# Key compression of a three-layer kernel with its blocks stationary in 64x32 tiles, and 1 MB of late weights loaded earlier

## What is computed

```python
def compress(kv, w1, w2, pe):                    # CMP_BLOCK 32, CMP_STRIDE 16, Dh 64, G 2
    B, T, G, Dh = kv.shape
    nc = (T - CMP_BLOCK) // CMP_STRIDE + 1       # 15 blocks
    idx = jnp.arange(nc)[:, None] * CMP_STRIDE + jnp.arange(CMP_BLOCK)[None, :]
    blocks = kv[:, idx] + pe[None, None, :, None, :]
    blocks = jnp.swapaxes(blocks, 2, 3).reshape(B, nc, G, CMP_BLOCK * Dh)
    return jax.nn.gelu(blocks @ w1) @ w2         # w1 is 2048 x 128, once for keys, once for values

def second_block(...):
    ...
    kc = compress(k_c...); vc = compress(v_c...)
    h = h + mix @ w_out[i]
    h = h + moe(rmsnorm(h, ln2[i]), w_router[i], ...)                               # 32 experts, top 4
    h = h + (p[i] @ w_ple[i]) * jax.nn.sigmoid(rmsnorm(h, ln_ple[i]) @ w_ple_gate[i])   # the last embedding
    return rmsnorm(h, ln_f)
```

## Time and profile before

| | |
|---|---|
| median of 3 runs | 1890.81 us (1889.72 to 1892.59) |
| profiled execution, own time | 1888.31 us |
| its span in the profile | 1886.4 us |
| TensorE busy with matmuls | 1733.7 us (92%) |
| VectorE / ScalarE busy | 744.8 us (39%) / 460.9 us (24%) |
| bytes moved | 549.43 MB, 291 GB/s over the span |
| granted TensorE clock, mean | 0.962 of full |

### The profile page before, as it was taken

The page is one execution under the profiler, slowest core; times in us unless marked ns, Lnnn a source line. Parts: engine busy times, 40 slices in busy tenths (PEclk is TensorE's granted clock), DMA queues, the critical chain, the costliest instruction groups (busy, mean ns, idle before and its releaser), DMA issues.

```text
span 1886.4 us, 23728 instructions
## 1 busy us (share of the span) xinstructions
PE 1733.7 (92%) x9692; PEld 1095.8 (58%) x9692; DVE 744.8 (39%) x1138; ACT 460.9 (24%) x725; POOL 13.1 (1%) x19
## 2 busy tenths in 40 slices
PE   8999999899999999999999889888898888977986
PEld 5799899797489989876544234333343333423332
DVE  3655567864365552153322222222222222213236
ACT  1544446522144441144222001000010100101003
POOL 0000000100000000000000000000000000000000
PEclk9999999999999999899899999999998999989998
DMA  9544443301354462213899999999999999999993
GB/s 395 211 196 196 192 154 135 134 1 77 146 234 179 178 232 113 80 45 132 331 428 427 428 428 428 428 428 425 429 428 429 428 427 428 428 427 428 427 428 160
DMA packets 41960, 549.43 MB, mean 291 GB/s; under 512 B 4824, under 2 KB 4984, under 8 KB 8728
## 3 DMA queue, kind: packets, MB, share of 16 engines
q1 hardware_dynamic: 39720, 540.45, 68.7%
q0 software_dynamic: 1872, 6.82, 1.0%
q10 hardware_dynamic: 288, 1.05, 0.1%
HBM read 545.12 MB, written 3.18 MB: 291 GB/s over the span
## 4 chain that ended last, share of the span: by engine, by line
PE 76%; DMA 17%; DVE 3%; ACT 2%; issue 1%; SPq 0%; DVEq 0%; ACTq 0%
DMA ring<-experts_dram 17%; PE ps L536 6%; PE ps L2186 6%; PE ps L2209 5%; PE ps L2231 5%; PE ps L2270 4%; PE ps L649 3%; PE ps L651 3%; PE ps L650 3%; PE ps L725 3%; PE ps L724 3%; PE ps L723 3%; PE ps L1241 3%; PE ps L2243 3%; PE ps L1456 2%; PE ps L2323 2%
## 5 line engine op out<-in xcount | busy, mean ns | idle before, releaser
L778 DVE TENSOR_TENSOR ring_split<-ring,ring_split 128x1024 fp32r<-128x1024 f32 x156 | 187.1, 1222 | 126.5 <-ACT ring_split L830 126.5
L2209 PE MATMUL ps<-ring,arena 128*32 128x512 f32 x1152 | 160.6, 709 | 81.6 <-DMA ring<-experts_dram 81.6
L2703 DVE TENSOR_SCALAR arena<-ps 128x512 f32<-128x512 f32 (+1 forms) x38 | 21.5, 566 | 495.1 <-PE ps L2209 201.4
L830 ACT CAST ring_split<-ring 128x1024 fp32r<-128x1024 f32 x156 | 160.6, 1047 | 165.0 <-PE ps L725 93.0
L2231 PE MATMUL ps<-ring,arena 128*128 128x512 f32 x384 | 168.6, 597 | 0.0
L3009 ACT ACTIVATE arena<-arena 128x512 f32<-128x512 f32 (+1 forms) x38 | 20.2, 530 | 574.6 <-DVE arena L2703 574.6
L2209 PEld LDWEIGHTS ps<-ring,arena 128*32 128x32 f32 x1152 | 42.0, 127 | 188.7 <-issue 182.5
L723 PE MATMUL ps<-arena_split,ring_split 128*128 128x256 f32 x512 | 145.3, 284 | 0.0
L725 PE MATMUL ps<-arena_split,ring_split 128*128 128x256 f32 x512 | 144.8, 283 | 0.0
L724 PE MATMUL ps<-arena_split,ring_split 128*128 128x256 f32 x512 | 144.4, 282 | 0.0
L2231 PEld LDWEIGHTS ps<-ring,arena 128*128 128x128 f32 x384 | 73.5, 192 | 88.8 <-issue 87.2
(11 more groups left out here) (435 smaller groups left out, 2501.3 us busy)
## 6 DMA issues: line engine op xcount, KB each, us to landing
ring<-experts_dram SPq DMA_DIRECT2D x192, 2048.0 KB, 20.0
ring<-weights_dram SPq DMA_DIRECT2D x55, 2048.0 KB, 11.4
row_buf<-rows_dram POOLq DMA_DIRECT2D x13, 512.0 KB, 9.0
ring<-heads_dram SPq DMA_DIRECT2D x4, 1024.0 KB, 4.8
ring<-weights_dram SPq DMA_DIRECT2D x3, 1024.0 KB, 11.5
tab<-tables_dram SPq DMA_DIRECT2D x1, 2160.5 KB, 31.4
tab<-weights_dram SPq DMA_DIRECT2D x1, 1536.0 KB, 25.7
gate_mid<-weights_dram SPq DMA_DIRECT2D x1, 1536.0 KB, 28.0
```

What stands on the lines that cost most here:

```text
L778: V.tensor_tensor(low, raw, high, ALU.subtract).then_inc(sem("part_low"), 1)
L830: A.copy(split_buffer(MLP_SPLIT_SLOT, buffer)[0], raw).then_inc(sem("part_high"), 1)
L2209: ins = T.matmul(view(bank(0)[TINY * q:TINY * q + TINY], (2, 256)), xs_of(4 * c + d, j)[:, 0:TINY], w[q // 2][:, d, :, 256 * (q % 2):256 * ...
```

## The change

Two edits. **First**, the operands of the compression's first product change places. The 32 columns of `cmp_in` of one position (30 blocks and 2 columns set to zero) are stationary, and the 128 columns of weights move. Keys and values use different row halves, and four successive positions use four different column groups of 32, so eight tiles of 64x32 take turns. Position `i` adds into partitions `32 * (i % 4)` onwards, so that four partial sums of 32x128 stand below one another. VectorE copies them out of PSUM (`cmp_part`), and a new `pe_compress_sum`, placed behind the first of the four outputs of the fox keys, adds the four and turns the result in one product for keys and one for values, with the table `own_expert` (1 where the partition modulo 32 is the column) moving. The gelu reads that result. **Second**, the load of the last embedding's weights stands ahead of the wait for `router_ids`, with a wait of its own for `router_psum`.

```diff
-        cmp_in = scratch(5696, 32, 30)
+        cmp_in = scratch(5696, 32, 32)
...
+        cmp_part = view(m_small[:, 0:256], (2, P))
...
             for r in range(4):
+                if r == 1:
+                    pe_compress_sum(pe)
                 m = turned(ps[:, 0, r * SEQ:(r + 1) * SEQ], w, 512, lambda a: a[:, r * P:(r + 1) * P])
...
-                    m = V.tensor_tensor(cmp_in[:, 16 * q:16 * q + 16, 15 * g:15 * g + 15], tokens_,
-                                        spread(pe_cols[:, 16 * q:16 * q + 16], 15), ALU.add)
-            m.then_inc(flag_up("cmp_in"), 1)
+                    V.tensor_tensor(cmp_in[:, 16 * q:16 * q + 16, 15 * g:15 * g + 15], tokens_,
+                                    spread(pe_cols[:, 16 * q:16 * q + 16], 15), ALU.add)
+            V.memset(cmp_in[:, :, 30:32], 0.0).then_inc(flag_up("cmp_in"), 1)
...
             V.tensor_copy(cumT, ps[0:8, 1, 512:768]).then_inc(sem("fox_cum"), 1)
+            v.wait_ge(*flag("cmp_part_psum"))
+            V.tensor_copy(cmp_part, view(ps[:, 3, :], (2, 512))[:, :, 0:P]).then_inc(flag_up("cmp_part"), 1)
...
             for i in range(32):
+                at = 32 * (i % 4)
                 for kv in range(2):
                     rows_ = slice(64 * kv, 64 * kv + 64)
-                    m = T.matmul(ps[:, 3, 512 * kv:512 * kv + 30], w[rows_, i * P:(i + 1) * P], cmp_in[rows_, i, :],
-                                 start=(i == 0), stop=(i == 31))
+                    m = T.matmul(ps[at:at + 32, 3, 512 * kv:512 * kv + P], cmp_in[rows_, i, :], w[rows_, i * P:(i + 1) * P],
+                                 start=i < 4, stop=i >= 28, skip_group_check=True)
+            m.then_inc(flag_up("cmp_part_psum"), 1)
+
+        def pe_compress_sum(pe):
+
+            pe.wait_ge(*flag("cmp_part"))
+            for kv in range(2):
+                m = T.matmul(ps[:, 3, 512 * kv + P:512 * kv + P + 32], cmp_part[:, kv, :], table("own_expert"), start=True, stop=True)
             m.then_inc(flag_up("cmp_hid_psum"), 1)
...
-                A.activation(hid[:, kv, :, 0:15], view(ps[:, 3, 512 * kv:512 * kv + 30], (2, 15)), ACT.Gelu_apprx_tanh)\
+                A.activation(hid[:, kv, :, 0:15], view(ps[:, 3, 512 * kv + P:512 * kv + P + 30], (2, 15)), ACT.Gelu_apprx_tanh)\
                  .then_inc(sem("cmp_hid"), 1)
...
                     sp.dma_start(parts[TILES + t], pre_low[t].bitcast(F32)).then_inc(sem("parts_kept"), 16)
+                sp.wait_ge(*flag("router_psum"))
+                sp.dma_start(w_ple2, weights[places["unit"]["ple2"], :, 0:2048]).then_inc(sem("ple2_loaded"), 16)
             sp.wait_ge(*flag("router_ids"))
             e = expert_at(TINY_1)
             for r, chunk in enumerate((A, B, A + 1, B + 1)):
                 load(CHUNKS + r, CHUNKS + r, e, chunk)
-            if n == 0:
-                sp.dma_start(w_ple2, weights[places["unit"]["ple2"], :, 0:2048]).then_inc(sem("ple2_loaded"), 16)
```

More of the change, by code:

```diff
@@ L46 @@
         "gdn_o1_psum", "att_kv_psum", "att_nat_psum", "att_qf_psum", "fox_cum_psum",
-        "cmp_hid_psum", "fox_rows1_psum", "cmp_kv_psum", "fox_rows0_psum", "cmp_score_psum", "cmp_pT_psum", "cmp_o_psum", "router_psum",
+        "cmp_part_psum", "cmp_hid_psum", "fox_rows1_psum", "cmp_kv_psum", "fox_rows0_psum", "cmp_score_psum", "cmp_pT_psum", "cmp_o_psum", "router_psum",
         "router_rank_psum", "router_wT_psum", "router_ids_psum", "router_sorted_psum",
@@ L52 @@
         "gdn_wT", "cmp_clear", "att_kv", "att_nat", "cmp_in", "fox_f", "fox_lf",
-        "cmp_hv4", "att_kf", "cmp_kcc", "cmp_vblk", "fox_bias", "cmp_diff", "cmp_prob", "cmp_pT", "cmp_o",
+        "cmp_part", "cmp_hv4", "att_kf", "cmp_kcc", "cmp_vblk", "fox_bias", "cmp_diff", "cmp_prob", "cmp_pT", "cmp_o",
         "router_top", "router_chosen", "router_rank", "router_weight", "router_perm", "router_wT", "router_ids",
```

## The result

The change takes 1881.07 us (median of 5 runs, 1878.98 to 1881.23), the kernel before 1890.60 beside it (5 runs, 1889.72 to 1892.59). The ratio is 0.9945, with an interval of 0.9930 to 0.9959: 9.5 us less. The forecast was 12.3 us less, 1878.5, with a range of 1874.5 to 1884.0.

The account below looks back on a forecast made before the run. The engines were taken to set the pace up to the experts, the DMA engines from there on. Gains of 9.8 us (compression path) and 2.45 (1 MB load) made 12.3, so 1890.8 became 1878.5 us, range 1874.5 to 1884.

Parts of the forecast that it names:

- eight tiles work at once: Compression's first product: column and row tiles overlap in full, so the stage takes 1.9 us instead of 10.92.
- the 9.8 of the path: TensorE's path through compression, sum and fox keys: 26.3 us before, 16.5 after, a gain of 9.8 us.
- the copy: VectorE's copy of the partial sums: hidden behind the first quarter of the fox keys, about 0.7 us if uncovered.
- rival 2: Compression stage: start rate or tiles limit it to 3.5 to 6.9 us instead of 1.9; time 1882.5; chance 0.11.
- rival 1: Compression: the clock falls once all the same, costing 1.75 us, up to 3.5; time 1881; chance 0.17.
- The fall behind the scores: Block scores: 3.32 us of thin work brought a clock fall, costing the fox values behind it 1.75 us.
- The 1 MB: Last embedding's load, moved ahead of the full expert stream: gain 2.45 us at 428 GB/s, bounds 0 and 2.5.
- Rival 3: Expert stream: the 1 MB load was free already, so moving it gains 0; time 1881; chance 0.08.
- the forecast's own sign: Expert stream: prediction wrong if first unit's issue to last landing isn't 2.4 us shorter.
- all that follows until 936 us: Compression to the expert stream: everything there hangs on TensorE, VectorE and ScalarE and moves along with the 9.8 us.
- theory A: Whole kernel, stated after the result: both terms are as forecast; what is missing is where the clock falls elsewhere.
- theory B: Whole kernel, stated after the result: a term is smaller than forecast, and one pair of profiles hides it.

Follow-up runs that it names:

- experiment 1: The changed kernel with the 1 MB load put back behind the four units, so the first edit alone: 1888.24 us, ratio 0.9973 to the kernel before.
- experiment 5: The changed kernel run again, unedited, beside the kernel before: 1884.32 us, ratio 0.9958.
- experiment 6: The first edit alone (small tiles, 1 MB load not moved), run a second time unaltered: 1883.76 us, ratio 0.9963 to the kernel before.
- experiment 2: The kernel before with only the 1 MB load moved, so the second edit alone: 1890.01 us, ratio 0.9991 to the kernel before.
- Experiment 8: The changed kernel with all key products ahead of the value products, so only four column tiles overlap: 1879.32 us, ratio 0.9935 to the kernel before.
- experiment 3: The changed kernel with all positions in one column group, so only two row halves overlap: 1890.08 us, ratio 0.9986 to the kernel before.
- experiment 7: The changed kernel with 2.62 MB (mid gate's weights and the 1 MB load) put into the expert stream: 1890.47 us, ratio 0.9985 to the kernel before.
- experiment 10: The changed kernel with the summing products ahead of all fox keys, so nothing covers VectorE's copy: 1881.18 us, ratio 0.9942 to the kernel before.

## Why the prediction was right, and where it was short

**The compression: right.** 1.96 us were measured for the 1.9 of "eight tiles work at once", with starts in groups of eight, and 9.78 for the 9.8 of the path. That the path fits to a tenth is in part luck: both profiles happened to lose 1.7 us behind the scores. Other profiles with the new compression give 8.1 (experiments 1 and 5, 135.15) to 11.4 us (experiment 6, 131.82) for the same stretch. Without the clock's losses, before and experiment 2 need 136.4 us there, the change and experiments 1, 5 and 6 131.7 to 131.8. So 4.7 us of the gain are work, and the rest, 3.4 to 6.8 us, is clock. Experiment 8 (3.24 us, forecast for four tiles: 3.5) and experiment 3 (7.1, forecast 7.0) bear out both ends of the step. So does the copy: covered in the change, 0.63 us when it isn't, and 0.7 in the forecast.

**How fast records start.** L1606's 128 records start within 1.8 us (768.3 to 770.1), 14 ns apart on the mean. So the 54 ns of rival 2 were no limit on starts, as the forecast took them. By the 25 ns between starts that the Trainium skill states ("TensorE: Matmul & The Clock Gate", the section on the gap of 56 ns) the stage would be an estimated 3.2 us, and this trace doesn't agree: it is 1.96.

**The clock in the compression: right.** It read 1.00 from 765 to 785 us in the change, and rival 1 didn't come. Experiment 3 adds which part of the gain it is: 4.3 of the 9.8 us, net of the sum.

**The fall behind the scores: right in size, wrong as a fixed thing.** Where it came in the kernel before it cost the 1.75 us that it was priced at (8.83 us, and 7.13 without it). But the forecast read from one profile that 3.32 us of such work bring a fall. In the ten profiles with the old order of the scores it cost nothing in four, 1.7 us in four and 3.4 in two, behind the same 32 records. In both profiles with the pairing there was none. None in two of two, against none in four of ten, is too little to show that the pairing took it away.

**The 1 MB: the mechanism right, the size a little under.** 2.45 us were forecast. The landing comes 1.8 us sooner (mean of eight profiles with the load moved, 917.85, against 919.66 of the three without), and the runs of experiment 2 give 1.9. The dose of experiment 7 gives 2.5 us for a load of this size. Rival 3, that it was free, is out by experiment 7. Single profiles of the eight lie between 916.98 and 918.48, so whether 1.8 or 2.45 is right stays open. By the forecast's own sign (the last landing 2.4 us sooner) this term fell short: 2.17 us in the pair of profiles, 1.8 by the means. Counted to the end of the kernel it is worth 0.8 us in the pair with the old compression (949.3 behind the first issue, not 950.1). With the new one it is 2.3: 949.8 in the mean of seven profiles, 952.1 in that of the two without the move.

**The sum: the step that fell short.** The forecast let "all that follows until 936 us" move along unchanged, and took one profiled execution for the kernel. By the means of the runs, each beside runs of the kernel before, the change gains 10.4 us the first time and 8.0 the second, so 9.2 where 12.3 were forecast. Three pieces of the missing 3.1 us can be read from the table:

- the fall near the router. When it begins some 4.5 us behind the router's start it lasts 20.5 us and costs 3.6 us up to the first unit. Of the eight profiles with the new compression and the old scores, four had it early (experiments 1, 3, 5 and 10); of the two with the old compression, none. The four profiles of the change and of the first edit alone have it twice, so the share doesn't hang on the kernels of experiments 3, 8 and 10. If it comes half the time, it takes 1.8 us off the mean gain, which is an estimate from these counts;
- the load, 0.65 us less than its term;
- last landing to end: 30.9 and 31.0 us (30.90 for before, 949.26 - 918.29 for experiment 2) with the old compression, 31.4 to 32.8 in the ten others, about 1.0 us more. The clock doesn't explain it: in the 30 us behind the last landing it costs 6.4 and 6.1 us with the old compression and 5.0 to 6.1 with the new one. No run was made on this piece, and its cause is open.

Together 3.5 us, for a gap of 3.1. So theory A accounts for an estimated 1.8 us of it and theory B for the 0.65 of the load; the last piece is neither's, and it is not shown that these three are the whole gap. The falls ahead of the compression (1.7 to 8.5 us) and behind the scores (0 to 3.4) are draws of the same kind. They widen the spread, and with three or five runs they can move a median.

What isn't shown is why the new compression should bring the early fall at the router more often. Two profiles of the old one are few. In its favour the kernel before also spreads less: 1.5 us standard deviation over 48 runs, against 2.5 for 10 runs of the change and 3.9 for 11 of the first edit alone. No run set the position of that fall on its own.

**The best version** is the change with the scores paired. It gains 13.1 and 11.1 us by the means, against 10.4 and 8.0 of the change, though the two were never run side by side. Over ten runs of each, means of 1880.0 and 1882.1 us are 2.1 us apart; the standard deviations (1.7 and 2.5) leave that just beyond what chance gives. Its trace is the firmer ground: 3.0 us less from compression to router than in the profile of the change, in both profiles (1.4 against experiment 6, which has no fall there), of which a later fall takes back 2.0 (28.08 us from router to first unit instead of 26.12, though 1.7 less than the 29.75 of the early kind).

## What to carry to other kernels

A product that moves few columns for each stationary load can be turned round, so that the small operand is stationary in a small tile. Here row and column tiles then worked at once when neighbouring records used different ones, and a 0/1 product added the partial sums for about half a microsecond. Price a thin stage by the clock behind it as well as by its own length. Give the falls that stand elsewhere on the path a term of their own, with both positions as its bounds: here they came to several microseconds, which differed between profiles of the same work. When an edit is worth less than the spread of one program, read its stage in the trace and run the unaltered kernels again: experiment 1 alone would have halved a gain that the trace showed in full.

## What was not expected

- Eight 64x32 tiles overlap nearly in full: 128 records of 128 columns in 1.96 us, 3.24 with four tiles, 7.1 with two. Each halving of the tiles costs a factor of 1.65 first and then 2.2.
- A stage on a quarter of the array (experiment 3, 7.1 us) kept the clock at 1.00, while half of the array with 30 moving columns was followed by 10.2 us at the lower level (1.2 GHz) in one profile and 13.7 in the other. Behind 3.3 us of the scores with 16 columns stood 0, 3.4 or 6.8 us at that level. Paired, the same 32 records in 1.96 us were followed by none in two profiles.
- The falls differ between profiles of the same work, in steps: at 265, 294 and 365 us they cost between 1.7 and 8.5 us together, behind the scores 0, 1.7 or 3.4, and the one at the router lasts 10.2, 17.1 or 20.5 us. Added up, that would cover the spread of up to 11 us between runs of one kernel (experiments 6 and 7).
- A DMA that is issued 16 us ahead of a full stream was worth no more than its bytes at the stream's rate (428 GB/s): 1.8 us at the last landing, where 2.45 were worked out, and in one pair of profiles only 0.8 at the end of the kernel.
